# Expert choice in a transformer kernel: the places of the second half's top values found eight rounds at a time on 128 partitions

## Chip, cores and metric

The kernel runs on one core of one Trainium2 chip, in one launch. The metric is device time in microseconds (us), start to end of the whole program; lower is better.

## What is computed

The program is a whole block of a network (latent attention beside a linear recurrence, a routed mixture of experts) followed by two transformer layers, one with windowed attention (called ec0 here) and one with a gated linear recurrence (ec1). Each of these two layers ends in an expert-choice mixture of experts, and the change lies in how its experts choose their tokens. Cut to that:

```python
def expert_choice_moe(x, w_router, w_gate_up, w_down):      # x: 1024 tokens x 1024
    cap = CAPACITY_FACTOR * S // N_EXPERTS_2                # 128
    aff = jax.nn.softmax((x @ w_router).astype(jnp.float32), axis=-1)   # 16 experts
    gates, idx = lax.top_k(jnp.swapaxes(aff, 1, 2), cap)
    xs = x[bi, idx]
    g, u = jnp.split(jnp.einsum('becd,edf->becf', xs, w_gate_up), 2, axis=-1)
    out = jnp.einsum('becf,efd->becd', jax.nn.silu(g) * u, w_down) * gates[..., None]
    return jnp.zeros_like(x).at[bi, idx].add(out)
```

Each of 16 experts takes the 128 tokens with its highest affinity, runs them through its own weights, and adds the results, times their gates, to those tokens' rows. Everything is float32.

## The kernel before

Each transformer layer ends in `layer_tail` (L2818), which runs two phases. `product_and_choose` (L2829, tensors named ec0p_ and ec1p_) multiplies the mixer's output by w_out, adds the residual, norms it, computes the router's affinities and lets the experts choose. `choice_phase` (L3087, ec0e_ and ec1e_) then gathers, computes and scatters for one expert after another; its expert loop takes most of the layer's time. At the end of the first phase all engines meet at a barrier and GpSimd clears the phase's semaphores (L84, L85), so no engine starts the second phase before the choice is complete.

`product_and_choose` goes over eight tiles of 128 tokens. Per tile TensorE does 16 matmuls of 128x128 by 128x512 in two halves (`product`, L2896), transposes the normed tile (L2905), multiplies it by the router's weights (`logits`, L2916, eight matmuls with 16 columns), and transposes the 128x16 affinities into 16x128 (`turn_aff`, L2923). VectorE does the sums, the norm and the softmax, and `keep_aff` (L3038) copies the transposed affinities into `affT`: `affT[0]` holds tokens 0 to 511, `affT[1]` tokens 512 to 1023, experts on 16 partitions. Semaphores tie the engines together; each engine runs its own list of instructions in the written order. `V.link` (L49) makes VectorE wait for its own instruction before the next.

The choice works on the two halves separately. `rounds(part, ns)` (L3040) does, for each n, one round on 16 partitions: `max` gives the eight highest of 512 values (L3045), `max_index` their places (L3046), and `match_replace` overwrites them with -1 in a second buffer (L3050), the input of the next round. Sixteen rounds sort out the top 128 of a half. The rounds of the first half are spread between the tiles by the table `between` (L3052). The rounds of the second half can start only when the last tile's affinities are there, and run one after the other (L3072). Then the two sorted lists are merged (L3074 to L3080: slot s of the merged choice is the larger of the s-th highest of the first half and the s-th lowest of the second half's list), on 16 partitions with 128 slots each; TensorE transposes indices and gates to slots on partitions (L2940, L2941); and three copies make `idx` and `gate` (L3082 to L3084).

In `choice_phase` GpSimd copies a column of `idx` and gathers 128 rows by an indirect DMA (L3154), TensorE transposes them (`turn_x`, L3200), VectorE copies them (L3338), and TensorE runs the expert's matmuls (`quarter`, L3220, and L3248). Weights of expert 0 are loaded on SyncE's queue during the first phase (L2880 and L2882 for the gate and up weights, L2885 for the down weights).

Of the kernel before, what the change touches and what calls it, by code (L numbers as in the profile page):

```python
# [13 lines left out]
P = 128  # L14
# [2814 lines left out]
def product_and_choose(nc, ph, aT, ident, wo_in, ln_mix, w_router, x_dram, mid_dram, acc_dram, gate, idx, weights):  # L2829
# [16 lines left out]
    top_i = [ph.sb(f"top_i{n}", [E2, CAP], U32) for n in range(2)]  # L2846
    top_f = [ph.sb(f"top_f{n}", [E2, CAP]) for n in range(2)]
    first = ph.sb("first", [E2, CAP])
    best = ph.sb("best", [E2, CAP])
    best_i = ph.sb("best_i", [E2, CAP])  # L2850
# [5 lines left out]
             "a_kept acc_ready tops f_psum").split()  # L2856
    (consts, half_psum, summed, nm_ready, sq_done, ms_ready, root, o_half, x_psum, xT_ready, l_psum, sh_ready, exp_done, aff_ready, a_psum,
     a_kept, acc_ready, tops, f_psum) = [ph.sem(n) for n in names]
# [4 lines left out]
    halves = [slice(h * HALF, (h + 1) * HALF) for h in range(2)]  # L2863

    with nc.Block() as block:
# [22 lines left out]
        def _(pe):  # L2888
# [48 lines left out]
            turn_aff(NT - 1)  # L2937
            pe.wait_ge(exp_done, NT)
            pe.wait_ge(tops, 1)
            nc.tensor.transpose(pl[:, 0:E2], best_i[:, :], ident[0:E2, 0:E2])  # L2940
            nc.tensor.transpose(pl[:, E2:2 * E2], best[:, :], ident[0:E2, 0:E2]).then_inc(f_psum, 1)  # L2941

        @block.scalar
        def _(act):
# [44 lines left out]
            store_acc(NT - 1)  # L2989
            for u in range(2):  # L2990
                act.wait_ge(o_out[u], 16 * (NT // 2))
                act.wait_ge(acc_out[u], 16 * (NT // 2))

        @block.vector
        def _(dve):
# [44 lines left out]
            def rounds(part, ns):  # L3040
                if ns[0] == 0:
                    dve.wait_ge(a_kept, 4 * part + 4)
                for n in ns:
                    eight = slice(8 * n, 8 * n + 8)
                    V.link(nc.vector.max(top[part][:, eight], affT[part][:, n % 2, :]))  # L3045
                    found = nc.vector.max_index(top_i[part][:, eight], top[part][:, eight], affT[part][:, n % 2, :])  # L3046
                    if n == CAP // 8 - 1:
                        V.link(found)
                    else:
                        V.link(nc.vector.match_replace(affT[part][:, (n + 1) % 2, :], top[part][:, eight], affT[part][:, n % 2, :], -1.0))  # L3050

            between = {5: (range(0, 0), range(0, 4)), 6: (range(4, 6), range(6, 10)), 7: (range(10, 12), range(12, 15)), 8: (range(15, 16), range(0, 0))}  # L3052
            total(0, 0)
            total(0, 1)
            for s in range(1, NT + 1):
# [5 lines left out]
                if s in between and between[s][0]:  # L3061
                    rounds(0, between[s][0])
# [4 lines left out]
                if s in between and between[s][1]:  # L3067
                    rounds(0, between[s][1])
            softmax(NT - 1)
            V.link(nc.vector.tensor_copy(top_f[0][:, :], top_i[0][:, :]))  # L3070
# [827 lines left out]
```

## Time and profile before

| | us |
|---|---|
| median of 3 runs | 4551.51 |
| lowest and highest of them | 4548.59, 4554.1 |
| the profiled execution, its own time | 4548.02 |
| span of the profiled execution, first to last instruction | 4546.3 |
| TensorE busy | 4190.0 (92% of the span) |
| VectorE busy | 1632.0 (36%) |
| ScalarE busy | 1074.1 (24%) |
| GpSimd busy | 269.4 (6%) |
| mean granted TensorE clock, share of full | 0.968 |

The profile is of one execution. Its engines are PE (TensorE's matmuls), PEld (TensorE's weight loads, which overlap them), DVE (VectorE), ACT (ScalarE), POOL (GpSimd) and SP (SyncE). Busy time counts an engine's instructions, not its waits.
### The profile page before, as it was taken

The page shows a single profiled execution, that of the slowest core. Times are in us where ns is not written, and L with a number is a line of the kernel's source. Part 1 is how long each engine was busy: PE and PEld are TensorE (multiplying, and loading weights), DVE is VectorE, ACT ScalarE, POOL GpSimd, SP SyncE. Part 2 cuts the span into 40 slices and gives each one's busy share as a digit, 9 for nine tenths or more (in the row PEclk, how much of TensorE's full clock was granted, in tenths as well). Part 3 has the DMA queues.
Part 4 walks back from the last instruction along what each step waited for, and adds up shares of the span by engine and source line. Part 5 has one row for each costly group of instructions (what it writes and reads, how often), then busy time and mean ns, then how long its engine had stood idle before and what let it go on. Part 6 is the DMA issues. An engine that isn't in the chain of part 4 may idle for free. (4 is left out here: it accounts for less than half of the span.)

```text
span 4546.3 us, 61110 instructions
## 1 busy us (share of the span) xinstructions
PE 4190.0 (92%) x23074; PEld 2174.5 (48%) x23075; DVE 1632.0 (36%) x3011; ACT 1074.1 (24%) x1849; POOL 269.4 (6%) x305
## 2 busy tenths in 40 slices
PE   8999997888999799989899599999899995999998
PEld 5555446775444444444555244444444452444443
DVE  4554564443422422224665310101446445110113
ACT  1354224443100011111453100000346331000002
POOL 0000002220000011110000000000000000000000
PEclk9999999999999899999999799999999997999999
DMA  2300155332212399961114498888611143889896
GB/s 85 151 21 31 46 193 138 81 77 97 74 31 88 113 362 356 359 238 37 38 36 164 173 321 311 315 314 311 217 37 33 56 176 131 310 320 316 307 322 245
DMA packets 409406, 799.36 MB, mean 176 GB/s; under 512 B 140656, under 2 KB 275824, under 8 KB 376304
## 3 DMA queue, kind: packets, MB, share of 16 engines
q1 hardware_dynamic: 380240, 696.41, 43.7%
q0 software_dynamic: 16848, 61.35, 4.8%
q10 hardware_dynamic: 12112, 38.67, 2.1%
q8 instruction: 152, 2.49, 0.2%
q14 instruction: 54, 0.44, 0.0%
HBM read 678.57 MB, written 117.44 MB: 175 GB/s over the span
## 5 line engine op out<-in xcount | busy, mean ns | idle before, releaser
L3220 PE MATMUL ec0e_pg<-ec_wg,ec0e_xT 128*128 128x512 f32 x1024 | 444.0, 594 | 2.1 <-DVE ec0e_xT L3338 2.1
L3220 PE MATMUL ec1e_pg<-ec_wg,ec1e_xT 128*128 128x512 f32 x1024 | 443.7, 594 | 2.1 <-DVE ec1e_xT L3338 2.1
L3220 PEld LDWEIGHTS ec0e_pg<-ec_wg,ec0e_xT 128*128 128x128 f32 x1024 | 195.5, 191 | 247.7 <-issue 247.7
L3220 PEld LDWEIGHTS ec1e_pg<-ec_wg,ec1e_xT 128*128 128x128 f32 x1024 | 195.4, 191 | 247.5 <-issue 247.5
L3248 PE MATMUL ec0e_py<-late_wd,ec0e_hidT 128*128 128x512 f32 x512 | 226.2, 595 | 3.4 <-ACT ec0e_hidT L3274 3.4
L3248 PE MATMUL ec1e_py<-late_wd,ec1e_hidT 128*128 128x512 f32 x512 | 226.2, 595 | 3.4 <-ACT ec1e_hidT L3274 3.4
L3574 PE MATMUL lrui_pA<-lrui_xT,lrui_w 128*128 128x512 f32 x512 | 221.3, 593 | 1.4 <-DVE lrui_xT L3725 1.4
L759 PE MATMUL front_pz<-h_h_all,h_w 128*128 128x512 f32 x480 | 209.5, 594 | 3.2 <-PEq L85 3.2
L3346 DVE TENSOR_TENSOR ec1e_hid<-ec1e_sg,ec1e_pg 128x512 f32<-128x512 f32 x32 | 22.0, 688 | 401.0 <-ACT ec1e_sg L3269 401.0
L3346 DVE TENSOR_TENSOR ec0e_hid<-ec0e_sg,ec0e_pg 128x512 f32<-128x512 f32 x32 | 22.0, 688 | 399.8 <-ACT ec0e_sg L3269 399.6
L3269 ACT ACTIVATE ec1e_sg<-ec1e_pg 128x512 f32<-128x512 f32 x32 | 19.2, 599 | 604.4 <-PE ec1e_pg L3220 604.4
L3269 ACT ACTIVATE ec0e_sg<-ec0e_pg 128x512 f32<-128x512 f32 x32 | 19.1, 598 | 603.6 <-PE ec0e_pg L3220 603.6
L3574 PEld LDWEIGHTS lrui_pA<-lrui_xT,lrui_w 128*128 128x128 f32 x512 | 97.4, 190 | 124.0 <-issue 124.0
L1063 POOL TENSOR_TENSOR wkv_a_l<-wkv_a_raw,linear_tab 128x512 f32<-128x512 f32 x80 | 106.3, 1360 | 757.0 <-ACT wkv_a_raw L1082 757.0
L3248 PEld LDWEIGHTS ec0e_py<-late_wd,ec0e_hidT 128*128 128x128 f32 x512 | 94.9, 190 | 113.8 <-issue 113.8
L3248 PEld LDWEIGHTS ec1e_py<-late_wd,ec1e_hidT 128*128 128x128 f32 x512 | 94.9, 190 | 113.8 <-issue 113.8
L759 PEld LDWEIGHTS front_pz<-h_h_all,h_w 128*128 128x128 f32 x480 | 90.6, 190 | 120.1 <-issue 120.1
L509 PE MATMUL mlaa_pS<-mla_kT,mla_qT 96*128 96x512 f32 x256 | 128.4, 625 | 4.8 <-ACT mlaa_probs L572 2.7
L3603 PE MATMUL lrui_pB<-late_wd,lrui_gw 128*128 128x512 f32 x256 | 116.1, 612 | 6.5 <-ACT lrui_buf L3641 6.5
L2896 PE MATMUL ec1p_po<-late_wd,layers_aT 128*128 128x512 f32 x256 | 115.6, 607 | 5.1 <-PEq L85 5.1
L1909 PE MATMUL route_po<-h_h_all,mixed_mixT 128*128 128x512 f32 x256 | 115.5, 606 | 4.8 <-PEq L85 4.8
L2491 PE MATMUL gqap_pq<-late_wd,gqap_xT 128*128 128x512 f32 x256 | 115.0, 604 | 1.3 <-DVE gqap_xT L2569 1.3
(653 smaller groups left out, 6392.3 us busy)
## 6 DMA issues: line engine op xcount, KB each, us to landing
ec_wg<-in_moe_w_gate_up_dram SPq DMA_DIRECT2D x256, 1024.0 KB, 6.5
late_wd<-in_moe_w_down_dram SPq DMA_DIRECT2D x256, 512.0 KB, 4.5
moe_wb<-in_w_dram SPq DMA_DIRECT2D x32, 1024.0 KB, 9.6
h_h_all<-in_w_dram SPq DMA_DIRECT2D x32, 1024.0 KB, 11.8
yb<-mlaa_zero SPq DMA_DIRECT2D x1, 16384.0 KB, 42.6
moe_w2b<-in_w_dram SPq DMA_DIRECT2D x16, 1024.0 KB, 11.7
mixed_mixT<-in_w_dram SPq DMA_DIRECT2D x16, 1024.0 KB, 13.4
yb<-ahead_rows ACTq DMA_DIRECT2D x32, 512.0 KB, 7.3
```

Of the source, the lines that this page charges most:

```text
L509: m = nc.tensor.matmul(pS[:, u % 2 * 2 + j, :], q_all[:, head, tile * P:(tile + 1) * P], k_all[:, head, j * HALF:(j + 1) * HALF], start=Tr ...
L759: m = nc.tensor.matmul(pz[q % 2][:, half * HALF:(half + 1) * HALF], w[:, q % U, k, :], hT[:, k, half * HALF:(half + 1) * HALF], start=k == ...
L1063: nc.gpsimd.tensor_tensor(grid(a_l[:, n, :]), grid(a_raw[:, :]), mask(n + 1), ALU.mult).then_inc(a_masked, 1)
L1909: m = nc.tensor.matmul(po[:, t % 2, halves[h]], mT[:, k, t * P:(t + 1) * P], wo[:, k, halves[h]], start=k == 0, stop=k == KD - 1)
L2491: m = nc.tensor.matmul(pq[:, b, :], xT[:, i % 2, k, :], w, start=k == 0, stop=k == KD - 1)
L2896: m = nc.tensor.matmul(po[:, t % 2, halves[h]], aT[:, k, t * P:(t + 1) * P], wo[:, k, halves[h]], start=k == 0, stop=k == KD - 1)
L3220: return nc.tensor.matmul(pg[:, b, :], xT[:, k, :], wg[:, k, b * HALF:(b + 1) * HALF], start=k == 0, stop=k == KD - 1)
L3248: m = nc.tensor.matmul(py[:, b * HALF:(b + 1) * HALF], hidT[:, k, :], wd[:, k, b * HALF:(b + 1) * HALF], start=k == 0, stop=k == KD - 1)
L3269: nc.scalar.activation(sg[:, half * HALF:(half + 1) * HALF], pg[:, half, :], ACT.Silu).then_inc(silu, 1)
L3346: nc.vector.tensor_tensor(hid[:, cols], sg[:, cols], pg[:, 2 + half, :], ALU.mult).then_inc(hid_ready, 1)
L3574: m = nc.tensor.matmul(pA[:, bank, :], w[:, q % W_RING, k, :], xT[:, k, halves[h]], start=k == 0, stop=k == KD - 1)
L3603: m = nc.tensor.matmul(pB[:, at, :], gw[:, u % 2, z, k, c, :], xc[:, u // 2 * 2 + c, halves[h]], start=c == 0, stop=c == 1)
```

## The change

Only `product_and_choose` changes. The rounds of the first half stay as they are. In each round of the second half VectorE keeps `max` and `match_replace` and leaves out `max_index`. Instead, TensorE copies the round's input (16x512) and its eight values (16x8) onto partitions 16r to 16r+15 of two PSUM tiles, r being the round's number in its group of eight, by matmuls with a shifted identity `to_lane` that accumulate over the group (`to_lanes`). After eight rounds ScalarE copies the 128x8 values to SBUF, and one `max_index` on 128x512 finds the places of all eight rounds (`places`). VectorE converts them and spreads them with a mask `own` to 128x(8x16); eight accumulating matmuls per group with shifted tables `to_slot` bring them to slots on partitions, in reversed order (`to_slots`). `places(0)` stands on VectorE after round 11, `to_slots(0)` on TensorE after round 13's copies. The merge is done on 128 partitions by 16 experts: the first half's lists are transposed early and copied by ScalarE (`low`), the second half's values are reversed (`top_r`) and transposed (`high`). VectorE builds the tables at the start of the phase (`make_tables`). The phase has 31 named semaphores where it had 19.

```diff
@@ -2843,24 +2843,44 @@
...
+    top_f = ph.sb("top_f", [E2, CAP])
+    top_r = ph.sb("top_r", [E2, CAP])
...
+    to_lane = ph.sb("to_lane", [E2, 2 * P - E2])
+    to_slot = ph.sb("to_slot", [P, 2 * P - 57])
+    own = ph.sb("own", [P, E2])
+    group = ph.sb("group", [P, LANES])
+    needles = [ph.sb(f"needles{c}", [P, 8]) for c in range(2)]
+    place_i = [ph.sb(f"place_i{c}", [P, 8], U32) for c in range(2)]
+    place_f = [ph.sb(f"place_f{c}", [P, 8]) for c in range(2)]
...
+    best_i = ph.sb("best_i", [P, E2])
...
+
+    def lane_copy(c):
+        return po[:, 0, halves[c]]
...
+    def lane_needles(c):
+        return po[:, 1, c * HALF:c * HALF + 8]
+
+    high_i, high = pt[:, 0:E2], pt[:, HALF:HALF + E2]
 
     with nc.Block() as block:
 
@@ -2935,10 +2955,39 @@
             transposes(NT - 1)
             logits(NT - 1)
             turn_aff(NT - 1)
+
+            def to_lanes(n):
+                c, r = n // LANES, n % LANES
+                lanes = to_lane[:, P - E2 - E2 * r:2 * P - E2 - E2 * r]
+                if n:
+                    pe.wait_ge(staged, n)
+                else:
+                    pe.wait_ge(a_kept, NT)
+                nc.tensor.matmul(lane_copy(c), lanes, affT[1][:, n % 2, :], start=r == 0, stop=r == LANES - 1).then_inc(copied, 1)
+                pe.wait_ge(eights, n + 1)
+                nc.tensor.matmul(lane_needles(c), lanes, top[1][:, 8 * n:8 * n + 8], start=r == 0, stop=r == LANES - 1).then_inc(sent, 1)
+
+            def to_slots(c):
+                pe.wait_ge(spread_in, c + 1)
+                for k in range(8):
+                    at = 64 * c + k
+                    m = nc.tensor.matmul(high_i, to_slot[:, at:at + P], spread[c][:, k, :], start=c == 0 and k == 0, stop=c == 1 and k == 7)
+                m.then_inc(slots_in, 1)
+
             pe.wait_ge(exp_done, NT)
-            pe.wait_ge(tops, 1)
-            nc.tensor.transpose(pl[:, 0:E2], best_i[:, :], ident[0:E2, 0:E2])
-            nc.tensor.transpose(pl[:, E2:2 * E2], best[:, :], ident[0:E2, 0:E2]).then_inc(f_psum, 1)
+            pe.wait_ge(low_ready, 1)
+            nc.tensor.transpose(pl[:, 0:E2], top_f[:, :], ident[0:E2, 0:E2])
+            nc.tensor.transpose(pl[:, E2:2 * E2], top[0][:, :], ident[0:E2, 0:E2]).then_inc(low_psum, 1)
+            pe.wait_ge(summed, 2 * NT)
+            pe.wait_ge(tables, 1)
+            for n in range(ROUNDS):
+                to_lanes(n)
+                if n == ROUNDS - 3:
+                    pe.wait_ge(xT_ready, 2 * NT)
+                    to_slots(0)
+            pe.wait_ge(turned, 1)
+            nc.tensor.transpose(high, top_r[:, :], ident[0:E2, 0:E2]).then_inc(high_psum, 1)
+            to_slots(1)
 
         @block.scalar
         def _(act):
@@ -2987,6 +3036,11 @@
             nc.scalar.activation(warm[:, NT - 1:NT], ident[:, 0:1], ACT.Exp)
             exps(NT - 1)
             store_acc(NT - 1)
+            act.wait_ge(low_psum, 1)
+            nc.scalar.copy(low[:, :, :], pl[:, 0:2 * E2].rearrange("p (x e) -> p x e", x=2)).then_inc(low_kept, 1)
+            for c in range(2):
+                act.wait_ge(sent, LANES * (c + 1))
+                nc.scalar.copy(needles[c][:, :], lane_needles(c)).then_inc(needles_in, 1)
             for u in range(2):
                 act.wait_ge(o_out[u], 16 * (NT // 2))
                 act.wait_ge(acc_out[u], 16 * (NT // 2))
@@ -3037,19 +3091,50 @@
                 dve.wait_ge(a_psum, t + 1)
                 nc.vector.tensor_copy(affT[t // 4][:, 0, t % 4 * P:(t % 4 + 1) * P], pa[0:E2, 0:P]).then_inc(a_kept, 1)
 
-            def rounds(part, ns):
+            def rounds(ns):
                 if ns[0] == 0:
-                    dve.wait_ge(a_kept, 4 * part + 4)
+                    dve.wait_ge(a_kept, 4)
                 for n in ns:
                     eight = slice(8 * n, 8 * n + 8)
-                    V.link(nc.vector.max(top[part][:, eight], affT[part][:, n % 2, :]))
-                    found = nc.vector.max_index(top_i[part][:, eight], top[part][:, eight], affT[part][:, n % 2, :])
-                    if n == CAP // 8 - 1:
-                        V.link(found)
+                    V.link(nc.vector.max(top[0][:, eight], affT[0][:, n % 2, :]))
+                    found_low = nc.vector.max_index(top_i[:, eight], top[0][:, eight], affT[0][:, n % 2, :])
+                    if n == ROUNDS - 1:
+                        V.link(found_low)
                     else:
-                        V.link(nc.vector.match_replace(affT[part][:, (n + 1) % 2, :], top[part][:, eight], affT[part][:, n % 2, :], -1.0))
+                        V.link(nc.vector.match_replace(affT[0][:, (n + 1) % 2, :], top[0][:, eight], affT[0][:, n % 2, :], -1.0))
+
+            def make_tables():
+                nc.vector.memset(to_lane[:, :], 0.0)
+                nc.vector.memset(to_slot[:, :], 0.0)
+                V.link(nc.vector.reduce_sum(own[:, :], ident[:, :].rearrange("p (r e) -> p e r", e=E2), AX_X))
+                V.link(nc.vector.reduce_sum(group[:, :], ident[:, :].rearrange("p (r e) -> p r e", e=E2), AX_X))
+                V.link(nc.vector.tensor_copy(to_lane[:, P - E2:P], ident[0:E2, 0:E2]))
+                nc.vector.tensor_copy(to_slot[:, P - 57:P:8], group[:, ::-1]).then_inc(tables, 1)
+
+            def round_high(n):
+                if n == 0:
+                    dve.wait_ge(a_kept, NT)
+                else:
+                    dve.wait_ge(staged, n)
+                eight = slice(8 * n, 8 * n + 8)
+                nc.vector.max(top[1][:, eight], affT[1][:, n % 2, :]).then_inc(eights, 1)
+                dve.wait_ge(eights, n + 1)
+                if n < ROUNDS - 1:
+                    if n:
+                        dve.wait_ge(copied, n)
+                    nc.vector.match_replace(affT[1][:, (n + 1) % 2, :], top[1][:, eight], affT[1][:, n % 2, :], -1.0).then_inc(staged, 1)
+
+            def places(c):
+                dve.wait_ge(copied, LANES * (c + 1))
+                dve.wait_ge(needles_in, c + 1)
+                nc.vector.max_index(place_i[c][:, :], needles[c][:, :], lane_copy(c)).then_inc(found, 1)
+                dve.wait_ge(found, c + 1)
+                V.link(nc.vector.tensor_copy(place_f[c][:, :], place_i[c][:, :]))
+                nc.vector.tensor_tensor(spread[c][:, :, :], place_f[c][:, :].unsqueeze(2).to_broadcast([P, 8, E2]),
+                                        own[:, :].unsqueeze(1).to_broadcast([P, 8, E2]), ALU.mult).then_inc(spread_in, 1)
 
             between = {5: (range(0, 0), range(0, 4)), 6: (range(4, 6), range(6, 10)), 7: (range(10, 12), range(12, 15)), 8: (range(15, 16), range(0, 0))}
+            make_tables()
             total(0, 0)
             total(0, 1)
             for s in range(1, NT + 1):
@@ -3059,29 +3144,32 @@
                 if s >= 2:
                     softmax(s - 2)
                 if s in between and between[s][0]:
-                    rounds(0, between[s][0])
+                    rounds(between[s][0])
                 if s < NT:
                     total(s, 0)
                 if s >= 2:
                     keep_aff(s - 2)
                 if s in between and between[s][1]:
-                    rounds(0, between[s][1])
+                    rounds(between[s][1])
             softmax(NT - 1)
-            V.link(nc.vector.tensor_copy(top_f[0][:, :], top_i[0][:, :]))
+            nc.vector.tensor_copy(top_f[:, :], top_i[:, :]).then_inc(low_ready, 1)
             keep_aff(NT - 1)
-            rounds(1, range(CAP // 8))
-
-            low, high, low_i, high_i = top[0][:, :], top[1][:, ::-1], top_f[0][:, :], top_f[1][:, ::-1]
-            V.link(nc.vector.tensor_copy(top_f[1][:, :], top_i[1][:, :]))
-            nc.vector.tensor_tensor(best[:, :], low, high, ALU.max)
-            V.link(nc.vector.tensor_tensor(first[:, :], low, high, ALU.is_ge))
-            V.link(nc.vector.scalar_tensor_tensor(best_i[:, :], high_i, float(HALF), low_i, ALU.add, ALU.subtract))
+            for n in range(ROUNDS):
+                round_high(n)
+                if n == ROUNDS - 5:
+                    places(0)
+            nc.vector.tensor_copy(top_r[:, :], top[1][:, ::-1]).then_inc(turned, 1)
+            places(1)
+            dve.wait_ge(low_kept, 1)
+            dve.wait_ge(high_psum, 1)
+            nc.vector.tensor_tensor(gate[:, :], low[:, 1, :], high, ALU.max)
+            V.link(nc.vector.tensor_tensor(first[:, :], low[:, 1, :], high, ALU.is_ge))
+            dve.wait_ge(slots_in, 2)
+            V.link(nc.vector.scalar_tensor_tensor(best_i[:, :], high_i, float(HALF), low[:, 0, :], ALU.add, ALU.subtract))
             V.link(nc.vector.tensor_tensor(first[:, :], first[:, :], best_i[:, :], ALU.mult))
-            nc.vector.scalar_tensor_tensor(best_i[:, :], high_i, float(HALF), first[:, :], ALU.add, ALU.subtract).then_inc(tops, 1)
-            dve.wait_ge(f_psum, 1)
-            nc.vector.tensor_copy(idx[:, 0:E2], pl[:, 0:E2])
-            nc.vector.tensor_copy(idx[:, E2:E2 + 1], pl[:, 0:1])
-            nc.vector.tensor_copy(gate[:, :], pl[:, E2:2 * E2])
+            V.link(nc.vector.scalar_tensor_tensor(best_i[:, :], high_i, float(HALF), first[:, :], ALU.add, ALU.subtract))
+            nc.vector.tensor_copy(idx[:, 0:E2], best_i[:, :])
+            nc.vector.tensor_copy(idx[:, E2:E2 + 1], best_i[:, 0:1])
 
 
 def choice_phase(nc, outer, name, layers, x_dram, acc_dram, gate, idx, weights, ln_ffn, out_dram, steps, end):
```

## Rows read from the trace of the kernel before

**Rows 1.** The page, part 1: busy time, share of the span and instructions by engine.

```profile
PE 4190.0 (92%) x23074; PEld 2174.5 (48%) x23075; DVE 1632.0 (36%) x3011; ACT 1074.1 (24%) x1849; POOL 269.4 (6%) x305
```

**Rows 2.** Timeline of ec1p: start, us, engine, line, operation, tiles; round 0.

```profile
3785.25 0.68 DVE L3045 MAX8 ec1p_top<-ec1p_affT 16x8 f32<-16x512 f32 x1
3785.96 0.08 DVE L3046 MATCH_VALUE_LOAD ec1p_top_i<-ec1p_top,ec1p_affT 16x8 f32 x1
3786.04 0.67 DVE L3046 FIND_INDEX8 ec1p_top_i<-ec1p_top,ec1p_affT 16x8 uint32<-16x512 f32 x1
3786.64 0.06 DVE L3050 MATCH_VALUE_LOAD ec1p_affT<-ec1p_top,ec1p_affT 16x8 f32 x1
...
3787.40 0.68 DVE L3045 MAX8 ec1p_top<-ec1p_affT 16x8 f32<-16x512 f32 x1
```

**Rows 3.** Timeline of ec1p: last round, merge, and start of the next phase.

```profile
3817.55 0.68 DVE L3045 MAX8 ec1p_top<-ec1p_affT 16x8 f32<-16x512 f32 x1
...
3820.13 0.28 DVE L3079 TENSOR_TENSOR ec1p_first<-ec1p_first,ec1p_best_i 16x128 f32<-16x128 f32 x1
...
3821.27 0.17 DVE L3082 CAST ec_idx<-ec1p_pl 128x16 uint32<-128x16 f32 x1 [0.55 <-PE ec1p_pl L2941]
3821.36 0.15 DVE L3083 CAST ec_idx<-ec1p_pl 128x1 uint32<-128x1 f32 x1
3821.43 0.16 DVE L3084 COPY ec_gate<-ec1p_pl 128x16 f32<-128x16 f32 x1
3822.58 0.33 SPq L3131 DMA_DIRECT2D layers_gb<-in_ln_ffn_g_dram  x1
```

**Rows 4.** Windows: us, busy and count of PE, PEld, DVE, ACT, POOL, PEclk, DMA share, GB/s.

```profile
3779.70:3783.40 3.70, 3.61 (x17) 3.49 (x16) 0.06 (x1) 2.07 (x3) 0.00 (x0) 0.50 0.92 353
3785.20:3820.00 34.80, 0.00 (x0) 0.00 (x0) 33.60 (x83) 0.00 (x0) 0.00 (x0) 0.50 0.04 15
...
3834.60:3839.00 4.40, 4.36 (x7) 2.02 (x8) 0.00 (x0) 0.00 (x0) 0.00 (x0) 0.63 0.39 119
```

**Rows 5.** Timeline: ec0p's last round, and how two other phases end and begin.

```profile
2543.43 0.68 DVE L3045 MAX8 ec0p_top<-ec0p_affT 16x8 f32<-16x512 f32 x1
...
2547.31 0.17 DVE L3084 COPY ec_gate<-ec0p_pl 128x16 f32<-128x16 f32 x1
...
2364.97 0.42 DVE L2767 TENSOR_TENSOR layers_aT<-gqaa_ou,gqaa_pO 128x256 f32<-128x256 f32 x1 [2.45 <-ACT gqaa_ou L2719]
2366.16 0.81 SPq L2870 DMA_DIRECT2D ec0p_xt<-x  x2
2373.35 0.69 DVE L3004 SCALAR_TENSOR_TENSOR ec0p_r<-ec0p_xt,ec0p_po 128x512 f32<-128x512 f32 x1 [7.96 <-PE ec0p_po L2896]
...
3635.42 0.69 DVE L3798 TENSOR_TENSOR layers_aT<-lrui_gh,lrui_g 128x512 f32<-128x512 f32 x1
3637.38 0.82 SPq L2870 DMA_DIRECT2D ec1p_xt<-x  x2
```

**Rows 6.** Timeline of TensorE; the last row is of the chain that ended last.

```profile
3768.83 1.85 PE L2916 MATMUL ec1p_pl<-ec1p_w,ec1p_xT 128*128 128x16 f32 x16
...
3779.74 3.56 PE L2916 MATMUL ec1p_pl<-ec1p_w,ec1p_xT 128*128 128x16 f32 x16
...
3834.64 2.05 PE L3220 MATMUL ec1e_pg<-ec_wg,ec1e_xT 128*128 128x512 f32 x2 [2.05 <-DVE ec1e_xT L3338]
...
3879.82 27.47 PE ec1e_pg L3220 x64
```

**Rows 7.** The router's exponential on ScalarE, by tile: ns min/median/max.

```profile
L2958 ACT ACTIVATE ec1p_ex<-ec1p_pl,ec1p_soft x8: 273/273/274, 3673.4 to 3783.6; 128x16 f32<-128x16 f32 x8
```

**Rows 8.** Windows, columns as in rows 4: TensorE's clock under light and no load.

```profile
702.00:710.00 8.00, 4.94 (x161) 4.10 (x165) 3.27 (x8) 3.08 (x6) 0.00 (x0) 1.00 1.00 248
...
2190.00:2196.00 6.00, 2.61 (x14) 1.47 (x16) 2.58 (x10) 2.42 (x5) 0.00 (x0) 1.00 0.69 220
2196.00:2202.00 6.00, 3.60 (x12) 1.18 (x8) 2.65 (x11) 4.06 (x16) 0.40 (x1) 0.50 1.05 389
```

More of the change, by code:

```diff
@@ L2845, in product_and_choose @@
     top = [ph.sb(f"top{n}", [E2, CAP]) for n in range(2)]
[L2846 to L2850, printed above, removed]
+    top_i = ph.sb("top_i", [E2, CAP], U32)
+    top_f = ph.sb("top_f", [E2, CAP])
+    top_r = ph.sb("top_r", [E2, CAP])
+    ROUNDS = CAP // 8
+    LANES = P // E2
+    to_lane = ph.sb("to_lane", [E2, 2 * P - E2])
[5 more added lines that the diff above has]
+    place_f = [ph.sb(f"place_f{c}", [P, 8]) for c in range(2)]
+    spread = [ph.sb(f"spread{c}", [P, 8, E2]) for c in range(2)]
+    low = ph.sb("low", [P, 2, E2])
+    first = ph.sb("first", [P, E2])
+    best_i = ph.sb("best_i", [P, E2])
     po = ph.ps("po", [P, 2, D])
@@ L2855, in product_and_choose @@
     names = ("consts half_psum summed nm_ready sq_done ms_ready root o_half x_psum xT_ready l_psum sh_ready exp_done aff_ready a_psum "
-             "a_kept acc_ready tops f_psum").split()
+             "a_kept acc_ready low_ready low_psum low_kept tables staged eights copied sent needles_in found spread_in slots_in turned high_psum").split()
     (consts, half_psum, summed, nm_ready, sq_done, ms_ready, root, o_half, x_psum, xT_ready, l_psum, sh_ready, exp_done, aff_ready, a_psum,
-     a_kept, acc_ready, tops, f_psum) = [ph.sem(n) for n in names]
+     a_kept, acc_ready, low_ready, low_psum, low_kept, tables, staged, eights, copied, sent, needles_in, found, spread_in, slots_in, turned,
+     high_psum) = [ph.sem(n) for n in names]
     x_in = [ph.sem(f"x_in{u}") for u in range(2)]
```

## The prediction, before the changed kernel was run

> **What bounds the kernel now.** I read the page first: TensorE is busy 92% of the span and VectorE 36% [rows 1]. That average says nothing of the stage that changes, so I went to the timeline around the last affinities of each layer. From 3785.25 us VectorE works alone: sixteen rounds, then the merge, and the next phase's first instruction on SyncE comes at 3822.58 [rows 2, 3]. Over 34.8 us of that stretch the windows give VectorE 33.6 us and TensorE, ScalarE and GpSimd nothing [rows 4]. No transfer is due in it either: the DMA share is 0.04, so expert 0's weights are in. After it come a gather and the experts, which start whenever the choice ends. A microsecond taken out here is a microsecond of the kernel, once per layer: ec0p shows the same 4 us from its last `max` to its end (2543.43 to 2547.48) [rows 5]. The choice from the first of these `max` to the end of the gate's copy takes 3821.59 - 3785.25 = 36.3 us.
>
> **What goes.** A round lasts 3787.40 - 3785.25 = 2.15 us. The find and its load of eight values hold the engine from 3785.96 to 3786.64, 0.68 us [rows 2]. Fifteen rounds lose it before the sixteenth's `max`: 10.2 us. Rounds would then take 1.47 us. The additional satisfied wait (`copied`) per round I cost at nothing while TensorE keeps up. The sixteenth find, the merge and the transposes are 3821.59 - 3817.55 = 4.04 us from the last `max`'s start [rows 3]; all of that is replaced, and is set against the new tail.
>
> **What comes on VectorE before the last `max`.** `places(0)`: load and find 0.75 us, a wait 0.04, a cast 0.17, a wait 0.03, and the spread of 128 elements, which holds the next operation back by some 0.24 (a 16x128 product took 0.28, [rows 3]). Sum 1.23. The find is on 128 partitions from PSUM, which no row has: the same instruction on 16 partitions from SBUF took 0.67 [rows 2], and a sum on 128x512 out of PSUM 0.69 [rows 5]. I take 0.67; upward it could be 0.1 more, downward nothing. `make_tables` costs nothing: VectorE idles 7.96 us before its first sum in ec0p [rows 5], and seven small operations need some 2 us.
>
> **TensorE under the rounds.** This is the term that decides. A float32 matmul of 512 columns is two passes. At 2.4 GHz a pass takes 27.47/64 = 0.43 us; at 1.2 GHz one matmul's two passes took 2.05 us with start and drain, some 0.86 us each when they follow on [rows 6]. A matmul of few columns is two weight loads more than anything: sixteen records of the router took 1.85 us at 2.4 GHz and 3.56 us at 1.2, so 0.23 and 0.44 per matmul [rows 6]. No row has a 16-row stationary operand with 512 columns. From below, such a copy could cost no more than a short matmul, from above it is the full price of 128 rows; I take the full price, as the columns are the same. Per round TensorE then needs 0.86 + 0.2 + 0.15 for waits and the first load = 1.2 us at 2.4 GHz, which VectorE's 1.47 hides, and 1.7 + 0.4 = 2.1 us at 1.2 GHz, which it doesn't: `match_replace` waits for the copy before last (`copied`), and the round is back at about its old 2.15. 
>
> **Which clock.** The stretch begins at a granted clock of 0.50, and 3.7 us of router matmuls at 97% busy just before did not raise it [rows 4]. Under dense matmuls after a pause it rose within 3834.6 to 3839 [rows 4]. With copies at 1.2 GHz TensorE is busy without a gap from round 1 on, so I expect the clock up between round 2 and round 4. Once up, its load is (0.86 + 0.2)/1.47 = 72%. At 62% busy it stayed up over 8 us (702 to 710); at 44% it was gone by 2196 [rows 8]. 72% is on the side of the first. Until it rises the rounds are held up. Copy 0 and its values fill TensorE to 2.2 us, copy 1 to 3.9, and its semaphore lets round 2 replace at 4.1, where VectorE stands at 2 x 1.47 + 0.71 = 3.65: 0.45 us lost, 0.3 if the clock rises during copy 1. Copy 2 ends at 6.2 where VectorE, then at 4.8 + 0.7, stands at 5.6: with 0.62 more, 1.07 if it rises as late as round 4. I take 0.65.
>
> **The tail.** `to_slots(0)` puts sixteen records, 1.85 us, between round 13's and round 14's copies. TensorE finishes round 13's at 1.2 us after that round's `max` starts; then 1.85, twice 0.86 + 0.17, and 0.12 of drain end the last values at 5.1, which is 2.2 us after the sixteenth `max` starts (VectorE is there at 2 x 1.47). Without that backlog it would be 1.3. From 2.2: ScalarE's copy with waits 0.34 (0.27 for a 128x16 exponential, [rows 7]), find 0.75, cast 0.21, spread 0.31, giving 3.8; `to_slots(1)` 1.85 with its wait 0.1, 5.7; three steps of 0.22 on 128x16, 6.4; two casts, 0.24 (3821.27 to 3821.51, [rows 3]), 6.6. The gate and `first` are made under `to_slots(1)`, and the early transposes of the first half's lists under round 0. Against 4.04 the tail is 2.6 us longer. ScalarE's new copies stand behind its last store; only the phase's end is queued behind them.
>
> **The phase's end.** Twelve more semaphores are cleared. With about 17 semaphores the next phase starts 0.77 us after the last work (2365.39 to 2366.16), with 27 after 0.99 (3821.59 to 3822.58), with 37 after 1.27 (3636.11 to 3637.38) [rows 3, 5]. That is 0.02 to 0.03 each: 0.25 us, between 0 and 0.35. The change moves no DMA and passes no queue. The gather and the first expert keep their low clock, for TensorE is again idle for some 10 us before.
>
> **Sum per layer:** -10.2 + 1.23 + 2.6 + 0.25 + 0.65 = -5.5 us, twice: -11 us. The profiled execution (4548.02, span 4546.3) lies 3.5 us under the median of 4551.51. Its durations give the difference, which I take from the median: 4540.6 us. A measurement of this kernel can tell about 0.2%, 9.1 us, from no change. Bounds: without backlog (0.9), with lag at 0.3 and no cost for semaphores, -7 per layer, -14; with finds at 0.1 more each, lag 1.07 and transfers between engines 0.5 longer, -4.4, -8.8.
>
> **Rivals.**
> - *The clock stays at 1.2 GHz*, because 16 of 128 rows don't count as work: slower. TensorE sets the round: 16 x 2.1 + 3.56 for `to_slots(0)` = 37.2 us to the last values; then 1.7, `to_slots(1)` 3.6 and 0.9, 43.4; with waits and 0.25 for semaphores 44.1 against 36.3. That is +7.8 per layer, 4567 us. With both `to_slots` at 3.56 it loses once TensorE's round passes about 1.64 us. For it: 97% busy wasn't enough in 3.7 us, and a copy drives an eighth of the rows. Against: under every long dense stretch the clock rose. Chance 0.2. The skill (same page, "Part 1: The HAM clock gate") has the idle state throttled and activity as what releases it, without a word on rows; by it this rival falls, and rows 8 agree for matmuls of 64 rows.
> - *The clock rises and falls by turns*, as in 2190 to 2202 [rows 8]. About half the rounds then cost 0.63 more, 4.4 us, so -1.1 per layer: 4549 us, no change to be seen. Chance 0.17.
> - *The clock holds through the rounds but falls in the pause before `to_slots(1)`*, 1.7 us without a matmul: 1.7 more per layer, -3.8, 4544 us. Chance 0.13.
> - That it doesn't do what it says (the finds needed anyway, the copies off the path) has no separate case: the finds are gone from the rounds by the diff.
>
> **Numbers.** The forecast, clock up and held, has 0.5. Most of it, 0.42, is beyond 9.1 us; with a part of the third rival that is 0.45 faster. Slower is the first rival and an edge of the second, 0.21. The rest, 0.34, is within 0.2%. The range 4536 to 4555 takes in all but the first rival; the likeliest case alone gives 4536 to 4544.
>
> **What would show it.** Rounds at 1.47 us from `max` to `max` in the second half's sixteen, with a gap of 0.3 to 1.1 us in rounds 2 to 3 that ends on TensorE's copy. Copies at 0.43 us a pass and a granted clock of 1.00 in most of the stretch. From the sixteenth `max` to the last cast 6.6 us, with VectorE waiting for ScalarE at its start and for TensorE before the merge. A gap of 1.2 us between phases instead of 0.99. The prediction is wrong if the clock reads 0.50 throughout and rounds take 2.1 us, or if the find on 128 partitions is much over 0.7 us.

## The result, and the profile after

The median went from 4551.41 to 4569.32 us (six runs each on one chip; ratio 1.0043, 95% interval 1.0031 to 1.0055): slower by about 18 us, where 11 us faster was forecast and the range ended at 4555. The profiled execution took 4574.67 us (span 4572.9), the longest of its six. Its stages ahead of the change are already 7.5 us late (ec0p's first load is issued at 2373.71, before at 2366.16 [rows 5]), so durations are compared, not positions.

The page, part 1, answers to [rows 1]:

```profile
PE 4284.3 (94%) x23268; PEld 2228.5 (49%) x23269; DVE 1618.0 (35%) x2973; ACT 1075.6 (24%) x1855; POOL 269.9 (6%) x305
```

VectorE lost 14 us and TensorE gained 94. A mean over the span says no more than that; the timeline of ec1p in the changed kernel answers to [rows 2] for the rounds and to [rows 3] for the tail:

```profile
3803.80 0.68 DVE L3120 MAX8 ec1p_top<-ec1p_affT 16x8 f32<-16x512 f32 x1
...
3806.04 2.05 PE L2966 MATMUL ec1p_po<-ec1p_affT,ec1p_to_lane 16*128 16x512 f32 x2
...
3806.84 0.68 DVE L3120 MAX8 ec1p_top<-ec1p_affT 16x8 f32<-16x512 f32 x1
...
3807.89 0.43 PE L2968 MATMUL ec1p_po<-ec1p_top,ec1p_to_lane 16*128 16x8 f32 x2
...
3808.17 2.05 PE L2966 MATMUL ec1p_po<-ec1p_affT,ec1p_to_lane 16*128 16x512 f32 x2
3808.19 0.08 DVE L3125 MATCH_VALUE_LOAD ec1p_affT<-ec1p_top,ec1p_affT 16x8 f32 x1 [0.68 <-PE ec1p_po L2966]
3808.27 0.66 DVE L3125 MATCH_REPLACE8 ec1p_affT<-ec1p_top,ec1p_affT 16x512 f32<-16x512 f32 x1
3808.97 0.68 DVE L3120 MAX8 ec1p_top<-ec1p_affT 16x8 f32<-16x512 f32 x1
...
3833.84 3.60 PE L2974 MATMUL ec1p_pt<-ec1p_spread,ec1p_to_slot 128*128 128x16 f32 x16
...
3834.57 0.68 DVE L3120 MAX8 ec1p_top<-ec1p_affT 16x8 f32<-16x512 f32 x1
...
3842.11 0.09 DVE L3130 MATCH_VALUE_LOAD ec1p_place_i<-ec1p_needles,ec1p_po 128x8 f32 x1 [6.60 <-ACT ec1p_needles L3043]
3842.18 0.69 DVE L3130 FIND_INDEX8 ec1p_place_i<-ec1p_needles,ec1p_po 128x8 uint32<-128x512 f32 x1
...
3847.17 0.17 DVE L3168 SCALAR_TENSOR_TENSOR ec1p_best_i<-ec1p_pt,ec1p_low 128x16 f32<-128x16 f32 x1 [3.60 <-PE ec1p_pt L2974]
...
3847.88 0.15 DVE L3172 CAST ec_idx<-ec1p_best_i 128x1 uint32<-128x1 f32 x1
3848.92 0.33 SPq L3219 DMA_DIRECT2D layers_gb<-in_ln_ffn_g_dram  x1
```

From `max` to `max` are 3808.97 - 3806.84 = 2.13 us, as long as a round before (2.15), though the find is gone: `match_replace` waits 0.68 us, as long as the find was, for the copy of the round before. TensorE sets the round now: its two matmuls take 2.05 and 0.43 us and overlap a little, 2.13 from one copy's start to the next (3808.17 - 3806.04). From the sixteenth `max` to the end of the last cast are 3848.03 - 3834.57 = 13.46 us (4.04 before): 6.60 of it is VectorE waiting for the last values, which stand behind `to_slots(0)` and two copies, and 3.60 is `to_slots(1)`. From the first `max` to the end the choice takes 44.23 us in ec1p and 44.22 in ec0p; before it took 36.34 and 36.36. Windows of the same stretch, with the columns of [rows 4], say why:

```profile
3803.80:3812.00 8.20, 8.09 (x14) 4.10 (x15) 6.38 (x13) 0.19 (x1) 0.00 (x0) 0.50 0.17 67
3812.00:3833.00 21.00, 21.00 (x41) 10.90 (x40) 15.17 (x34) 0.17 (x1) 0.00 (x0) 0.50 0.00 0
```

TensorE works practically without a gap, and the granted clock stays at 0.50, which is 1.2 GHz, until the choice ends. The waits of VectorE in the choice, by line (sum, times, longest, in us):

```profile
DVE ec1p_affT L3125 <- PE ec1p_po L2966: 7.7, 12, 0.7
DVE ec1p_place_i L3130 <- ACT ec1p_needles L3043: 6.6, 1, 6.6
DVE ec1p_best_i L3168 <- PE ec1p_pt L2974: 3.6, 1, 3.6
```

The two choices give 7.89 + 7.86 = 15.75 us more than before. From the choice's end to the end of expert 0's 64 matmul records it takes 1.25 us more in ec0 and 0.2 in ec1. That makes 17.2 of the 17.9 by which the medians differ. What the trace doesn't tell is why the clock stayed down, and whether the low clock is what decided.

### The profile page after: what moved, and what is told of

Same layout as the page of the kernel before. It is cut to its first block and busy times, and to the rows that moved or that the text cites. A ratio compares the mean times of both kernels' runs of the same rounds, so it can differ in the third digit from the quotient of the medians.

```text
span 4572.9 us, 61500 instructions
## 1 busy us (share of the span) xinstructions
PE 4284.3 (94%) x23268; PEld 2228.5 (49%) x23269; DVE 1618.0 (35%) x2973; ACT 1075.6 (24%) x1855; POOL 269.9 (6%) x305
```

## The experiments

The theory: TensorE's clock isn't raised by matmuls whose operands stand on 16 partitions (16 rows); with more rows it would be, and the change would bring what was forecast. The rivals: the stretch as such doesn't get the clock (its load, memory traffic, the pauses and short matmuls between the copies), the zeros in the shifted identity keep it down, or the change's own sum is wrong. The runs were made on several chips, so each is compared with the kernel before on its own chip.

**Rows alone.** Two kernels are the kernel before with seventeen matmuls under the second half's rounds whose result nobody reads; they differ only in k, the number of partitions on which both operands stand.

```diff
+            for n in range(17):
+                nc.tensor.matmul(po[:, 0, 0:HALF], w[0:k, ...], gb[0:k, 0, 0:HALF], start=True, stop=True)
```

> The kernel before, with 17 matmuls of a 16-row stationary operand and 16x512 moving columns put on TensorE while VectorE does the second half's rounds; nobody waits for them and they wait for nothing. Theory 1 (the clock follows the rows in use): granted clock 0.50 through all 17, passes of 0.86 us, 29 us of them. Theory 2 (it is the waits and the short matmuls between the copies): the clock rises to 1.00 within the stretch, as under other dense matmuls, and the 17 take under 20 us. Theory 3 (it is the operand's zeros, a shifted identity): 1.00 too, for here both operands hold ordinary numbers. Either way the time stays that of the kernel before within 0.2%.

> The same 17 matmuls with 128 rows instead of 16. All theories: the clock rises to 1.00 after some matmuls and passes take 0.43 us; the contrast with the 16-row run is what counts. If the clock stays at 0.50 here as well, something else in this stretch holds it. Time that of the kernel before within 0.2%.

Windows of idle16, then of idle128:

```profile
3785.00:3800.00 15.00, 15.00 (x19) 6.11 (x19) 14.39 (x36) 0.06 (x1) 0.00 (x0) 0.50 0.09 36
3800.00:3812.00 12.00, 12.00 (x15) 4.66 (x14) 11.59 (x27) 0.00 (x0) 0.00 (x0) 0.50 0.00 0
```

```profile
3785.20:3788.00 2.80, 2.80 (x5) 1.25 (x5) 2.38 (x7) 0.25 (x1) 0.00 (x0) 0.50 0.46 187
3788.00:3790.00 2.00, 2.00 (x4) 0.81 (x3) 1.97 (x5) 0.00 (x0) 0.00 (x0) 0.56 0.02 4
3790.00:3792.00 2.00, 2.00 (x6) 0.95 (x5) 1.93 (x6) 0.00 (x0) 0.00 (x0) 1.00 0.00 0
```

Both keep TensorE busy without a gap from the same moment. With 16 rows the clock stays at 0.50 for all 29 us of it; with 128 it is up by 3790. In ec0p it is the same: 0.50 over 2513 to 2542 with 16 rows, 1.00 from 2514 on with 128. Their times were 4549.63 and 4549.88 us (one run each; before 4549.64 on that chip), since nobody waits for this work. So matmuls of 16 rows leave the clock down where the same matmuls of 128 rows raise it, with ordinary numbers in both operands and nothing of the change in the kernel.

**The change with more rows.** The copies' operands are widened; what stands in the added rows meets zeros in `to_lane`, so it doesn't enter the result.

```diff
-    affT = [ph.sb(f"affT{n}", [E2, 2, HALF]) for n in range(2)]
+    affT = [ph.sb("affT0", [E2, 2, HALF]), ph.sb("affT1", [ROWS, 2, HALF])]
-    to_lane = ph.sb("to_lane", [E2, 2 * P - E2])
+    to_lane = ph.sb("to_lane", [ROWS, 2 * P - E2])
+                nc.vector.memset(affT[1][:, :, :], 0.0)
+                nc.vector.memset(top[1][:, :], 0.0)
```

(`top[1]` likewise.) In rows128_data the memsets of `affT[1]` and `top[1]` are copies of real numbers; rows64_zero is rows128_zero with ROWS = 64.

> The changed kernel, with the copies' operands on 128 partitions instead of 16: the rows from 16 on are zero in both, so the results are the same. Theory 1 (rows in use): clock 1.00 in most of the rounds, rounds at 1.47 us, and the forecast's sum holds: some 5.5 us per layer under the kernel before, about 4540 us. Theory 2 (waits and short matmuls): as the changed kernel, 0.50 and 4569 us. Theory 3 (zeros): still 0.50, since seven eighths of the rows carry zeros; 4569 us.

> As the run with 128 rows of zeros, but the moving rows from 16 on hold the first token tile's numbers (the stationary rows stay zero, results the same). Theory 1: as that run, about 4540 us. Theory 2: 0.50 and 4569 us. Theory 3: between, if moving numbers count 1.00 and 4540 us, if only products that are not zero count 4569 us.

> The changed kernel with the copies' operands on 64 partitions, rows 16 to 63 zero. Between 16 rows (clock 0.50) and 128 rows (1.00): if the clock follows the rows in use and 64 are enough, as under the 64-row matmuls of the recurrence stage, 1.00 and a time near the 128-row run, about 4540 us; if all rows are needed, 0.50 and about 4568 us.

| | median, us | before on its chip | ratio (95%) | choice in ec0p, ec1p, us |
|---|---|---|---|---|
| before | 4551.41 | | | 36.36, 36.34 |
| changed | 4569.32 | 4551.41 | 1.0043 (1.0031 to 1.0055) | 44.22, 44.23 |
| rows128_zero | 4538.72 | 4549.64 | 0.9977 (0.9967 to 0.9986) | 31.89, 30.85 |
| rows128_data | 4541.68 | 4549.64 | 0.9983 (0.9974 to 0.9993) | 31.90, 30.86 |
| rows64_zero | 4574.39 (one run) | 4556.68 | | 44.23, 44.22 |

Timeline of ec1p in rows128_zero:

```profile
3781.92 0.68 DVE L3123 MAX8 ec1p_top<-ec1p_affT 16x8 f32<-16x512 f32 x1
3782.03 2.04 PE L2967 MATMUL ec1p_po<-ec1p_affT,ec1p_to_lane 128*128 128x512 f32 x2
...
3786.06 1.10 PE L2967 MATMUL ec1p_po<-ec1p_affT,ec1p_to_lane 128*128 128x512 f32 x2
3786.19 0.08 DVE L3128 MATCH_VALUE_LOAD ec1p_affT<-ec1p_top,ec1p_affT 16x8 f32 x1 [0.55 <-PE ec1p_po L2967]
...
3786.97 0.68 DVE L3123 MAX8 ec1p_top<-ec1p_affT 16x8 f32<-16x512 f32 x1
...
3788.46 0.68 DVE L3123 MAX8 ec1p_top<-ec1p_affT 16x8 f32<-16x512 f32 x1
...
3805.95 0.68 DVE L3123 MAX8 ec1p_top<-ec1p_affT 16x8 f32<-16x512 f32 x1
...
3808.49 0.09 DVE L3133 MATCH_VALUE_LOAD ec1p_place_i<-ec1p_needles,ec1p_po 128x8 f32 x1 [1.61 <-ACT ec1p_needles L3044]
...
3811.92 0.17 DVE L3171 SCALAR_TENSOR_TENSOR ec1p_best_i<-ec1p_pt,ec1p_low 128x16 f32<-128x16 f32 x1 [1.97 <-PE ec1p_pt L2975]
...
3812.63 0.14 DVE L3175 CAST ec_idx<-ec1p_best_i 128x1 uint32<-128x1 f32 x1
3813.67 0.33 SPq L3222 DMA_DIRECT2D layers_gb<-in_ln_ffn_g_dram  x1
```

The first copy takes 2.04 us as with 16 rows; the third takes 1.10. Rounds are 1.49 us (3788.46 - 3786.97). The whole change, with operands eight times as tall and not one instruction less, goes from 18 us slower to 11 us faster than before (8 with numbers in the added rows; the intervals overlap and the choices are equal, so zeros and numbers do the same). This also settles the rivals of waits, short matmuls and zeros: all of them are still there. Sixty-four rows don't help; the stretch of rows64_zero reads

```profile
3803.00:3848.00 45.00, 42.31 (x100) 25.07 (x100) 25.75 (x63) 0.86 (x4) 0.00 (x0) 0.50 0.03 12
```

These are always the same 64 partitions. The recurrence stage of the kernel before shows that 64-row matmuls aren't barred from a rising clock as such. A line of its timeline, then two windows:

```profile
699.14 1.98 PE L1245 MATMUL wkv_bF<-wkv_ar,wkv_kh 64*64 64x128 f32 x32
```

```profile
699.00:701.00 2.00, 2.00 (x37) 1.86 (x40) 0.00 (x0) 1.63 (x3) 0.24 (x1) 0.51 1.00 259
701.00:703.00 2.00, 1.20 (x68) 1.03 (x60) 1.29 (x2) 0.58 (x1) 0.00 (x0) 1.00 1.15 346
```

Here the clock rises just before 701, behind four 128-row transposes (from 698.10) and 64 records of 64 rows. But in this stage the heads stand in turn on partitions 0 to 63 and 64 to 127 (`rows = slice(64 * h, 64 * h + 64)`), so all 128 are in use. Whether the rows of one matmul count or the partitions used over a time was not tried apart.

**Less work for TensorE instead of a higher clock.** `once` copies the round-0 input alone onto all eight groups (in one 16-row matmul with the identity repeated) and sends only the values per round. It leaves out that chosen values are overwritten in the copy, so equal values chosen in different rounds would get the same place.

```diff
-                nc.tensor.matmul(lane_copy(c), lanes, affT[1][:, n % 2, :], start=r == 0, stop=r == LANES - 1).then_inc(copied, 1)
+                if n == 0:
+                    nc.tensor.matmul(lane_copy(0), every, affT[1][:, 0, :], start=True, stop=True).then_inc(copied, 1)
```

> The changed kernel (16-row operands) with one copy instead of sixteen: the first round's values are put on all eight groups of lanes at once, and all finds search that one copy. It leaves out the rounds' replaced values, so equal values chosen in different rounds would be given the same place. Theory (the changed kernel loses because sixteen copies at 1.2 GHz keep TensorE busier than VectorE's rounds): the clock still reads 0.50, but rounds fall to 1.5 us without it; the tail stays long, since to_slots takes 3.6 us at that clock. Per layer 15 x 0.68 = 10.2 us saved, places(0) 1.2, tail from the last max about 9.0 instead of 4.04: 4 us under the kernel before, about 4542 us. Rival (the finds on 128 partitions, the waits or the merge are what costs): the rounds would still be over 2 us, 4560 us or more.

4544.53 us against 4556.68 before on its chip, ratio 0.9975 (0.9964 to 0.9986); the clock is 0.50 throughout, rounds are 1.49 us, and the choice takes 32.6 us in both layers. So even at 1.2 GHz the idea pays 3.7 us a layer in the trace, once TensorE's part fits under VectorE's: what lost the time is the pair "copy of 512 columns in each round" and "low clock", not the low clock by itself.

**The backlog at the end.** slots_apart is rows128_zero with `places(0)` after round 8 and the sixteen small matmuls of `to_slots(0)` spread over rounds 9 to 15. warm is rows128_zero with seven useless 128-row matmuls ahead of the affinities of tile 6, to have the clock up for the router.

> The run with 128 rows of zeros, with places(0) after round 8 instead of 11 and the eight matmuls of to_slots(0) spread over rounds 9 to 15, two and then one at a time, in the 0.24 us that TensorE idles per round. Theory (the tail holds 0.9 us of backlog on TensorE behind to_slots(0)): the last values come 1.3 to 1.5 us after the sixteenth max starts instead of 2.2, and the layer is 0.8 us shorter, 1.6 in all, too little for the timed rounds to show. Rival (the backlog is hidden by other waits): the tail from the last max to the last cast stays at 6.8 us.

> The run with 128 rows of zeros, with seven 128-row matmuls of no use put on TensorE in the 7 us in which it waits for the last tile's norm, so that its clock doesn't fall. If the clock holds: the last tile's router matmuls take 1.85 us instead of 3.56, which VectorE waits for, and the rounds start at 2.4 GHz without the 0.6 us of lag: 2.3 us per layer, 4.6 in all, about 4534 us. Rival (the clock falls anyway in the gaps of 1 to 2 us around the router): no gain.

Before took 4556.68 us on their chip.

slots_apart: 4542.88 us, ratio 0.9973 (0.9962 to 0.9985). VectorE waits 0.64 us for the last values instead of 1.61. In ec1p it was given back: the clock fell within `to_slots(1)` (from 3814.36 on; 0.50 from 3815.5), which took 2.81 us instead of 1.96, so the choice took 30.80 us; in ec0p 30.41.

warm: 4542.79 us, ratio 0.9968 (0.9956 to 0.9981). The router's sixteen last records took 1.93 us in ec1p instead of 3.57. But then the clock fell as the rounds began, and ec1p's rounds waited 1.2 us for copies instead of 0.55. In ec0p of this execution, the longest of its six, it fell a second time, late in the rounds:

```profile
2530.00:2540.00 10.00, 7.71 (x25) 4.09 (x24) 9.55 (x23) 0.17 (x1) 0.00 (x0) 0.98 0.01 2
2540.00:2544.00 4.00, 4.00 (x15) 2.97 (x15) 3.30 (x8) 0.00 (x0) 0.00 (x0) 0.50 0.00 0
2544.00:2548.00 4.00, 4.00 (x11) 2.66 (x12) 0.00 (x0) 0.00 (x0) 0.00 (x0) 0.50 0.00 0
```

Just before, TensorE was 77% busy (7.71 of 10 us); in ec1p of the same execution the clock held with TensorE 85% busy (16.11 of 19 us, 3797 to 3816), in ec1p of rows128_zero with 80% (17.53 of 22). `to_slots(0)` then took 3.58 us, and this choice 37.36 us, more than before the change.

**Holding it at both ends.** held is slots_apart and warm together, with one more useless matmul behind the last router matmuls and one ahead of `to_slots(1)`. held_gather adds six ahead of the wait for the first gather. before_held is the kernel before with the useless matmuls alone (seven, one and six).

> The changed kernel with the copies' operands on 128 partitions, the second half of the rounds' first to_slots spread over rounds 9 to 15, seven useless matmuls of 128 rows before the affinities of tile 6 are turned, and one more each after the last router matmuls and ahead of the second to_slots. Theory (what held the time up in the earlier variants is only where TensorE pauses at a low clock): the granted clock is up from the router's last matmuls to the second to_slots; VectorE's wait for the last logits is 2.0 us instead of 4.0, the lag in rounds 1 to 3 goes from 0.6 to about 0.1, the wait for the last values is 0.6 instead of 1.6 and to_slots(1) takes 1.9; per layer -5.5 -2.0 -0.5 -0.9 = -8.9 us against the kernel before, about -18 us. Rival (one matmul is too little to carry the clock over the softmax or over the find): the clock reads 0.50 again in the first rounds or in to_slots(1), and the gain stays at that of the separate variants, -6 to -7 us per layer, -12 to -14 us.

> As held, and six useless matmuls of 128 rows on TensorE before it waits for the first gather. Theory: the clock is then up when expert 0 begins; its 64 matmul records of the gate product take 27.5 us instead of about 29 to 30, and its transposes about 1.0 instead of 2.0 us: 2.7 us per layer more, together about -23 us against the kernel before. Rival: the pause behind the six until the gathered rows are there lets the clock fall again, or the six end later than the gather and delay it: then the same time as held or up to 2 us per layer slower.

> The kernel before with the same useless matmuls: seven before the affinities of tile 6 are turned, one behind the last router matmuls, six before the wait for the first gather. Nothing of the change is in it. Theory (these gains are TensorE's clock at the two ends of the choice and have nothing to do with the choice's method): the rounds of the second half still take 2.15 us and 36.3 us for the choice, the router's wait is 2.0 us shorter and the first expert up to 2.7 us: -2.0 to -4.7 per layer, -4 to -9.4 us. If this kernel comes out within 2 us of held_gather, the changed method is worth nothing once TensorE is kept at its high clock.

| same chip, before 4548.80 | median, us | ratio (95%) | choice ec0p, ec1p | router to first `max` |
|---|---|---|---|---|
| held | 4533.17 | 0.9969 (0.9959 to 0.9979) | 30.65, 30.52 | 4.85, 3.79 |
| held_gather | 4530.77 | 0.9965 (0.9952 to 0.9979) | 29.81, 30.49 | 4.62, 3.80 |
| before_held | 4545.07 | 0.9995 (0.9986 to 1.0004) | 36.35, 36.36 | 4.64, 3.86 |

(Before, router to first `max` is 5.50 and 5.51.) The timeline of held, ec1p:

```profile
3777.47 1.93 PE L2937 MATMUL ec1p_pl<-ec1p_w,ec1p_xT 128*128 128x16 f32 x16 [0.44 <-ACT ec1p_xT L3025]
3779.25 1.10 PE L2961 MATMUL ec1p_po<-ec1p_gb,late_ident 128*128 128x512 f32 x2
...
3781.38 2.04 PE L2971 MATMUL ec1p_po<-ec1p_affT,ec1p_to_lane 128*128 128x512 f32 x2
...
3808.85 1.96 PE L2979 MATMUL ec1p_pt<-ec1p_spread,ec1p_to_slot 128*128 128x16 f32 x16 [0.21 <-DVE ec1p_spread L3144]
```

The second filler did its work (`to_slots(1)` 1.96 us, the wait for values 0.64, a tail of 5.85 us). The first didn't: the useless matmul at 3779.25 still runs at 2.4 GHz and the first copy, two microseconds later, takes 2.04 us; rounds 2 and 3 wait 0.68 and 0.54 us. In ec0p the clock fell still earlier, within the router's matmuls (0.91 over 2509.4 to 2511.0, then 0.50, TensorE busy without a gap). They took 2.39 us, and the useless matmul behind them 2.06, ahead of the last affinities: the router gave 0.65 us there and 1.72 in ec1p. The sum expected -8.9 a layer; the trace gives 1.72 + 5.82 = 7.5 in ec1p and 0.65 + 5.71 = 6.4 in ec0p, 13.9 together, and the ratio 0.9969 is 14.1 us (10 to 19). So the rival came true, at its price. In held_gather the six fillers didn't pay. In ec1 expert 0's transposes start 9.25 us after the choice instead of 7.88, take 1.04 us instead of 1.97, and its 64 records still take 29.40 us: the clock was up at their start and fell under them (0.71 over 3818 to 3820, 0.63 to 3823, then 1.00). From the choice's end to the end of those records it is 41.7 us, and 41.9 in held. before_held gains only what the router gives, 0.86 + 1.65 = 2.5 us, and its interval takes in no gain at all. So the fillers alone are not the gain: on one chip held stands 11.9 us below before_held, and held_gather, which has before_held's fillers too, 14.3; the choices of the traces of held and before_held differ by 5.70 + 5.84 = 11.5 us.

**Raising and holding.** `hold` is the kernel before with ten matmuls of 128 rows and then fourteen of 64 rows (ec0p) or 16 rows (ec1p) under the rounds.

> The kernel before with useless TensorE work under the second half's rounds, where nobody waits for it: ten matmuls of 128 rows, which in the earlier run raised the clock, and behind them without a pause fourteen of 64 rows in the first of the two layers, of 16 rows in the second. The time should be that of before. Theory A (rows count for raising the clock and for holding it alike): some microseconds after the narrow matmuls begin the granted clock falls to 0.50 in both layers, and one of them goes from 0.86 us to about 1.7 us. Theory B (narrow matmuls can hold a clock that is up and only fail to raise it, as the 64-row products at 702 to 710 us of the kernel before let one think): the clock stays at 1.00 to the last of them, 14 x 0.86 = 12 us. If 64 rows hold and 16 don't, the rows count by degrees.

It took 4544.03 us in its one run, and before 4556.93 in its one run on that chip. Nothing follows from the 12.9 us between two single runs: before ranged from 4541.71 to 4558.98 on the chip of held, and the choices of hold took 36.29 us in both layers, before's 36.36 and 36.34.

Windows of ec0p from the middle of the 64-row matmuls, then of ec1p before and behind the fall:

```profile
2520.00:2524.00 4.00, 4.00 (x11) 1.79 (x10) 3.86 (x11) 0.00 (x0) 0.00 (x0) 1.00 0.00 0
2524.00:2528.00 4.00, 4.00 (x10) 1.68 (x9) 3.86 (x9) 0.00 (x0) 0.00 (x0) 1.00 0.00 0
...
3794.00:3796.00 2.00, 2.00 (x6) 0.79 (x5) 1.93 (x6) 0.00 (x0) 0.00 (x0) 1.00 0.00 0
3796.00:3800.00 4.00, 4.00 (x7) 1.54 (x6) 3.86 (x11) 0.00 (x0) 0.00 (x0) 0.54 0.00 0
```

With 64 rows the clock stays up to the last matmul; with 16 it falls soon after 3796, with TensorE busy all the time, and stays down. The 48 records take 22.36 us in ec0p and 31.49 in ec1p. So 128 rows raise and hold, 64 rows (always the same 64 partitions) hold and in rows64_zero don't raise, 16 do neither: the rows count by degrees. hold and rows64_zero ran once each, and 64 rows without the copies' gaps were not tried as a way to raise the clock.

## Why the prediction was wrong

- **Which clock: the step that failed.** "With copies at 1.2 GHz TensorE is busy without a gap from round 1 on, so I expect the clock up between round 2 and round 4." The gap-free work was there (21.00 of 21 us), the clock wasn't: it read 0.50 to the end, so the copies stayed at 2.05 us and the round at 2.13. The sum took TensorE's busy time as all that raises its clock. The evidence was read too widely: the rise in [rows 4] is of 128-row matmuls, and the 702 to 710 of [rows 8] show a clock that was up already being *kept*, by 64-row products that stand in turn on both halves of the partitions, with 128-row transposes among them. The only 16-row matmuls in the trace of before are two transposes of some 0.25 us at the end of each choice.
- **The first rival, given 0.2, is what happened**, at its price: forecast rounds 2.1 us and +7.8 a layer, 4567 us; measured 2.13, +7.9 and 4569.32. Its reason, that 16 of 128 rows don't count as work, is borne out by idle16 and idle128, as far as that the number of rows decides; how the chip counts is not shown. The text held against it the Trainium skill ("TensorE: Matmul & The Clock Gate", "Part 1: The HAM clock gate"), where activity releases the throttle. If activity is busy time, idle16 doesn't agree (29 us at 100%, clock 0.50); that page says nothing of rows, and the rival was not to be struck by its silence. On the other point cited, that a short contraction costs as much as a full one ("Why this matters for your kernels"), the trace agrees: 2.04 us for a copy at the low clock, with 16 rows and with 128.
- **The rest of the sum stands, as rows128_zero shows.** In ec1p it took 36.34 - 30.85 = 5.49 us off (forecast 5.7 without the phase's end): rounds 1.49 us (1.47), TensorE's lag 0.55 (0.65), the last values 2.2 us behind the sixteenth `max` (2.2), the tail 6.82 (6.6), `find` on 128 partitions out of PSUM 0.68 to 0.69 (0.67). In ec0p it took 4.47 off, as the clock rose a little later (waits of 0.68 and 0.21) and fell within `to_slots(1)`, which took 2.69 us: the third rival, in part.
- **The phase's end: 0.25 us that aren't there.** In ec1p of the changed kernel it is 3848.92 - 3848.03 = 0.89 us from the last instruction to the next phase's first load, with twelve semaphores more; before it was 0.99. The three phase ends in [rows 3, 5] differ in more than their semaphores, and were read as a price for each.
- **The second rival, an unsteady clock, is real as well**, in ec0p of warm: it fell once before the rounds and once within them, at 77% busy. It was not what happened to the changed kernel.

## What to carry to other kernels

Ask of each TensorE stretch not only how busy it is but on how many partitions its operands stand. Small helper matmuls (copies, transposes, spreads) that come after a pause may run at 1.2 GHz for as long as they last. Either make their operands full height, with zeros, or see that their sum fits under the other engine at the low clock. Full height cost nothing here: a copy takes 2.04 us at the low clock with 16 rows and with 128, and the memsets (0.91 and 0.17 us) stand where VectorE still waits 4.49 us for TensorE afterwards. It is the difference between 18 us lost and 8 to 11 us gained, with the same instructions and two memsets more a layer. The 14 us of held take reordering and useless matmuls besides.

## What was not expected of the hardware

- Full occupation doesn't raise the clock when operands have 16 rows (29 us at 100% busy), nor did 64 rows, always the same, in rows64_zero (94% of 45 us at a mean of 0.50). With 128 rows it was up within 5 us of the first such matmul in both layers of idle128, and rows of zeros serve as well as rows of numbers.
- 64 rows, which didn't raise it there, held it for 12 us.
- A clock that is up falls at seams where TensorE has hardly paused: in ec1p of held between 3779.25 and 3781.38, where its longest wait is 0.18 us (0.96 us at 3775.86), and in ec0p within the router's matmuls without a pause. What in this stretch (outputs of 16 columns, transposes with 16 rows) lets it fall was not tried apart and stays open. So does where between 64 and 128 rows the rise begins.
- Expert 0's first matmuls don't profit from an earlier warm-up: its 64 records take 29.40 us (ec1) and 30.44 (ec0) in held_gather, and 29.29 to 30.71 in the other traces.
